# Triangular inverse of the delta rule: doubling levels on stacked 64-blocks instead of full 128-blocks

## The chip, the cores and the metric

The kernel runs on one NeuronCore of one Trainium2 chip. The metric is device time in microseconds (us), from one execution of the whole program. TensorE (PE) does the matrix products, VectorE (DVE) and ScalarE (ACT) the elementwise work, GpSimd (POOL) elementwise work and some DMA issues, SyncE (SP) issues the weight stream. Every matrix product of two float32 operands that this text speaks of shows in the trace as two passes, each one with its own weight load (LDWEIGHTS, the row PEld) and its own matmul record (the row PE).

## The reference, cut to what matters

Two layers of a hybrid block run in a loop, followed by a second block with gated linear attention, a convolution, differential attention and experts. Each of the two layers has a gated delta rule with 4 heads over 256 tokens. Its core is a unit lower-triangular solve:

```python
a_kk = jnp.where(strict, jnp.einsum('bhnid,bhnjd->bhnij', kb, k) * gamma, 0.0)
tri = a_kk + jnp.eye(C, dtype=f32)
rhs = jnp.concatenate([v * beta[..., None], kb * jnp.exp(G)[..., None]], axis=-1)
sol = lax.linalg.triangular_solve(tri, rhs, left_side=True, lower=True, unit_diagonal=True)
```

The kernel works with chunks of 128 tokens, so there are 4 heads x 2 chunks = 8 triangular matrices of 128x128 in each layer, and it builds their inverses. In the same stretch of the program runs the sliding-window attention of 8 heads of 64 features, which has nothing to do with the inverse and is woven into it.

## The kernel before

Weights stream through a ring of three 512 KB tiles; ACT and DVE split each tile into a high and a low part (L1586, L1824) and PE multiplies with three products per tile (L1246 to L1248). These products fill most of the program. Each engine executes its own list of instructions in order, and the lists are tied together by counting semaphores; nothing else sets the order.

The stretch that the change touches is the same in both layers, between the last input projection and the output projection. `bp` holds the 8 matrices (transposed, not yet masked), made by DVE at L2001 from the Gram products in PSUM (L1420) and decay factors times beta, which POOL multiplies at L2161. The inverse is then built by doubling, in `LEVELS` = 7 levels (0 to 6). At level `lev` the inverse of each diagonal block of size 2^lev is known, and blocks of twice the size are made of them:

- POOL makes the level's mask product `bl` (L2171): `bp` times a 0/1 matrix of constants ("level"), 8 matrices of 128x128 in one instruction (two instructions of four at level 0). `bl` has two buffers; from level 2 on POOL waits until level lev-2 is over.
- Level 0: PE turns `bl` (L1461, a product with the identity), DVE takes both `bl` and its turned form from the identity (L2035 and L2037). The results are `uinv` and `tinv`, the inverse and its transpose.
- Levels 1 to 6, first half, called X here: PE forms `bl` times `tinv` (L1470) into banks 6 and 7, ACT copies it to `xs` (L1736).
- Second half, called Y here: PE forms `uinv` times `xs` (L1479, not at level 6) and `xs` times `uinv` (L1481), and DVE subtracts them from `tinv` (L2042) and from `uinv` (L2043).

Each of these steps is done in two groups `g` of four matrices, one PSUM bank each. Between X and Y of each level, PE, DVE and ACT do one step `attend(i)` of the attention: the scores of head i (L1332, L1333, with 64 rows of the array), the transposes of head i-2 (L1327), and the values of head i-3 (L1450 to L1452, with 64 columns of the array). Thus the first two levels carry scores only, level 3 carries transposes too, and from level 4 on all three. After level 6 come the products of the recurrence (L1489 to L1517), again with `attend` steps between them.

POOL has one more piece of work in this stretch: behind the masks of levels 0 and 1 it forms `qg` and `kbg` (L2177 to L2180, twelve instructions) and issues two DMAs for `post_mix` and `post_ffn` (L2185), and only then the mask of level 2. DVE waits on `lev_y` and `tu_ready`, ACT on `lev_x`, PE on `bl_ready`, `tu_ready` and `lev_xs`.

Of the kernel before, what the change touches and what calls it, by code (L numbers as in the profile page):

```python
# [14 lines left out]
P = 128  # L15
# [16 lines left out]
LEVELS = 7  # L32

# [60 lines left out]
def columns(*widths):  # L94
# [10 lines left out]
    ("level", LEVELS * P), ("dilmask", 3 * P), ("causal", 3 * P), ("gmask", P),  # L105
# [50 lines left out]
def block_program(nc, xt, wtiles, consts, packa, packf, packb, packp, out):  # L156
    v, a, pl, t = nc.vector, nc.scalar, nc.gpsimd, nc.tensor
    ctx = ExitStack()
    with ctx:
# [74 lines left out]
        tinv, xs = (sq[:, 4 * i:4 * i + 4, :].rearrange("p a (u k) -> p (a u) k", k=P) for i in range(2))  # L234
        bl = y[:].rearrange("p (w a) (u k) -> p w (a u) k", w=2, k=P)
# [151 lines left out]
        lev_x, lev_xs, lev_y, tu_ready = sem("lev_x"), sem("lev_xs"), sem("lev_y"), sem("tu_ready")  # L387
        rec_pe, rec_act, rec_dve = sem("rec_pe"), sem("rec_act"), sem("rec_dve")
# [850 lines left out]
        def _(pe):  # L1239
# [99 lines left out]
            def layer(l):  # L1339
# [117 lines left out]
                pe.wait_ge(bc_dve, l * 4 + 4)  # L1457
                for g in range(2):
                    pe.wait_ge(bl_ready, l * (LEVELS + 1) + g + 1)
                    for u in range(4):  # L1460
                        mm = t.matmul(bank[g][:, u * P:(u + 1) * P], bl[:, 0, 4 * g + u, :], ident, start=True, stop=True)  # L1461
                    mm.then_inc(lev_x, 1)
                pe.wait_ge(tr_dve, l * 4 + 4)
                pe.wait_ge(tr_act, l * 4 + 4)
                for lev in range(1, LEVELS):
                    pe.wait_ge(bl_ready, l * (LEVELS + 1) + lev + 2)
                    for g in range(2):
                        pe.wait_ge(tu_ready, l * 2 * LEVELS + 2 * (lev - 1) + g + 1)
                        for u in range(4 * g, 4 * g + 4):
                            mm = t.matmul(bank[6 + g][:, u % 4 * P:u % 4 * P + P], bl[:, lev % 2, u, :], tinv[:, u, :],  # L1470
                                          start=True, stop=True)
                        mm.then_inc(lev_x, 1)
                    attend(lev - 1)
                    for g in range(2):

                        pe.wait_ge(lev_xs, l * 2 * (LEVELS - 1) + 2 * (lev - 1) + g + 1)
                        for u in range(4 * g, 4 * g + 4):
                            if lev < LEVELS - 1:
                                t.matmul(bank[g][:, u % 4 * P:u % 4 * P + P], uinv[:, u, :], xs[:, u, :],  # L1479
                                         start=True, stop=True)  # L1480
                            mm = t.matmul(bank[6 + g][:, u % 4 * P:u % 4 * P + P], xs[:, u, :], uinv[:, u, :],  # L1481
                                          start=True, stop=True)
                        mm.then_inc(lev_y, 1)
# [98 lines left out]
        def _(act):  # L1582
# [62 lines left out]
            def layer(l):  # L1645
# [87 lines left out]
                for lev in range(1, LEVELS):  # L1733
                    for g in range(2):
                        act.wait_ge(lev_x, l * 2 * LEVELS + 2 * lev + g + 1)
                        a.activation(xs[:, 4 * g:4 * g + 4, :], bank[6 + g][:, :].rearrange("p (u k) -> p u k", u=4),  # L1736
                                     ACT.Copy).then_inc(lev_xs, 1)
# [82 lines left out]
        def _(dve):  # L1820
# [84 lines left out]
            def layer(l):  # L1905
# [72 lines left out]
                for i in range(DNH + 1):  # L1978
# [14 lines left out]
                    if i < 0:  # L1993
# [7 lines left out]
                    v.tensor_tensor(bp[:, 2 * i:2 * i + 2, :], pair[:, :, 0, :],  # L2001
                                    bp[:, 2 * i:2 * i + 2, :], ALU.mult).then_inc(gram_used, 1)
# [22 lines left out]
                for lev in range(LEVELS):  # L2025
                    if lev >= 1:
                        attend(lev - 1)
                    for g in range(2):
                        us = slice(4 * g, 4 * g + 4)
                        t_ps = bank[g][:, :].rearrange("p (u k) -> p u k", u=4)  # L2030
                        u_ps = bank[6 + g][:, :].rearrange("p (u k) -> p u k", u=4)
                        if lev == 0:
                            eye = ident.unsqueeze(1).to_broadcast([P, 4, P])
                            dve.wait_ge(bl_ready, l * (LEVELS + 1) + g + 1)
# [336 lines left out]
```

## Time and profile before

| | us |
|---|---|
| median of 3 runs | 1341.01 |
| lowest, highest | 1338.49, 1342.27 |
| the profiled execution, its own time | 1337.07 |
| its span, first to last instruction | 1335.3 |
| busy share of the span: PE, DVE, ACT, POOL | 94%, 61%, 50%, 25% |

The rows below come from that profiled execution. Times in it are us from the start of the span. The stretch described above runs from about 122 to 192 us in the first layer and from about 538 to 608 us in the second. The page has a line "PEclk" with the granted clock of TensorE in each of 40 slices of the span, in tenths of full speed: 9 is full speed (2.4 GHz), and a lower digit is a slice in which the clock was at 1.2 GHz for some of the time. In other views the same share is 1.00 or 0.50. The chain of waits is the work that ended last, followed back from the last instruction to what released each step.

### The profile page before, as it was taken

To read this page: it belongs to the slowest core of one execution; us is meant where nothing else is said; L and a number is where in the kernel's file an instruction comes from. 1 tells how busy PE (TensorE), PEld (TensorE's weight loads), DVE (VectorE), ACT (ScalarE), POOL (GpSimd) and SP (SyncE) were. 2 spreads that over 40 slices of the span, in tenths; PEclk is the share of its full clock that TensorE was granted. 3 is DMA by queue.
4 is the path that set the end of the run, shared out by engine and by line. 5 is a ranking of instruction groups with operands and counts; after the bars stand their busy time and mean duration, and the time that the engine had idled before them with its cause. 6 is when DMAs were issued, how large, how long until landed. Compare 5 with 4: busy or idle time off the path is not lost.

```text
span 1335.3 us, 25081 instructions
## 1 busy us (share of the span) xinstructions
PE 1256.9 (94%) x8802; PEld 1163.0 (87%) x8802; DVE 817.2 (61%) x1293; ACT 664.0 (50%) x1085; POOL 328.5 (25%) x370
## 2 busy tenths in 40 slices
PE   8998898999997999899899999888789999999998
PEld 8997787999996999788899998788668889999997
DVE  5666546766666855555766666597355455555554
ACT  6654245655555664345555555583144444444442
POOL 2014301322222001510322222487200122222221
PEclk9999999999999999899999999998559889999999
DMA  6542003555553544003355555233103245555553
GB/s 240 166 152 80 32 4 109 199 187 181 182 188 112 171 147 145 32 1 108 123 181 182 187 188 188 80 127 111 48 1 110 80 142 188 185 182 185 186 187 128
DMA packets 49802, 181.12 MB, mean 136 GB/s; under 512 B 5568, under 2 KB 5728, under 8 KB 49600
## 3 DMA queue, kind: packets, MB, share of 16 engines
q1 hardware_dynamic: 48816, 176.98, 40.0%
q0 software_dynamic: 912, 3.16, 0.7%
q8 instruction: 46, 0.75, 0.2%
q14 instruction: 28, 0.23, 0.1%
HBM read 179.07 MB, written 1.05 MB: 135 GB/s over the span
## 4 chain that ended last, share of the span: by engine, by line
PE 83%; DVE 6%; POOL 4%; ACT 3%; issue 3%; DMA 0%; POOLq 0%; DVEq 0%; ACTq 0%; SPq 0%
PE bank L1246 22%; PE bank L1247 22%; PE bank L1248 22%; PE bank L1481 2%; PE bank L1470 1%; PE bank L1479 1%; PE bank L1305 1%; PE bank L1327 1%; POOL region L1186 1%; PE bank L1296 1%; POOL region L1161 1%; POOL region L1164 1%; PE bank L629 1%; PE bank L1333 1%; ACT w L1586 1%
## 5 line engine op out<-in xcount | busy, mean ns | idle before, releaser
L1824 DVE TENSOR_TENSOR w<-ring,w 128x1024 fp32r<-128x1024 f32 x330 | 412.1, 1250 | 224.4 <-ACT w L1586 224.2
L1246 PE MATMUL bank<-act,w 128*128 128x256 f32 x1728 | 498.8, 289 | 18.0 <-DVE act L1846 8.1
L1247 PE MATMUL bank<-act,w 128*128 128x256 f32 x1728 | 493.8, 286 | 0.0
L1248 PE MATMUL bank<-act,w 128*128 128x256 f32 x1728 | 493.6, 286 | 0.0
L1586 ACT ACTIVATE w<-ring 128x1024 fp32r<-128x1024 f32 x330 | 347.7, 1055 | 188.0 <-PE bank L1248 181.7
L1246 PEld LDWEIGHTS bank<-act,w 128*128 128x128 f32 x1728 | 336.6, 195 | 25.2 <-issue 11.3
L1247 PEld LDWEIGHTS bank<-act,w 128*128 128x128 f32 x1728 | 336.9, 195 | 2.3
L1248 PEld LDWEIGHTS bank<-act,w 128*128 128x128 f32 x1728 | 336.4, 195 | 0.0
L2094 DVE SCALAR_TENSOR_TENSOR region<-bank,pf,region 128x255 f32<-128x255 f32 (+1 forms) x176 | 84.8, 482 | 74.8 <-ACT region L1787 63.7
L1246 PE MATMUL bank<-w,hid 128*128 128x512 f32 x304 | 119.3, 393 | 3.9 <-POOL hid L2196 2.0
L1247 PE MATMUL bank<-w,hid 128*128 128x512 f32 x304 | 118.9, 391 | 0.0
L1248 PE MATMUL bank<-w,hid 128*128 128x512 f32 x304 | 118.3, 389 | 0.0
L1787 ACT ACTIVATE region<-bank,pf 128x256 f32<-128x256 f32 x88 | 49.6, 563 | 132.4 <-PE bank L1248 132.2
L2193 POOL TENSOR_TENSOR region<-region 128x256 f32<-128x256 f32 x44 | 65.0, 1478 | 180.7 <-DVE region L2094 146.9
L2142 POOL TENSOR_TENSOR h<-act 128x256 f32<-128x256 f32 x48 | 38.4, 839 | 257.5 <-DVE act L1846 257.4
L1246 PE MATMUL bank<-w,act 128*128 128x256 f32 (+1 forms) x208 | 71.9, 346 | 1.2 <-DVE w L1824 1.2
L1246 PEld LDWEIGHTS bank<-w,hid 128*128 128x128 f32 x304 | 57.3, 188 | 15.5 <-POOL hid L2196 2.8
L1247 PE MATMUL bank<-w,act 128*128 128x256 f32 (+1 forms) x208 | 69.6, 335 | 0.0
L1248 PE MATMUL bank<-w,act 128*128 128x256 f32 (+1 forms) x208 | 69.6, 335 | 0.0
L1248 PEld LDWEIGHTS bank<-w,hid 128*128 128x128 f32 x304 | 57.1, 188 | 12.3
L1247 PEld LDWEIGHTS bank<-w,hid 128*128 128x128 f32 x304 | 57.3, 188 | 9.7
L1199 POOL TENSOR_TENSOR region<-region 128x256 f32<-128x256 f32 x32 | 24.7, 772 | 154.7 <-DVE region L1110 154.7
(329 smaller groups left out, 1648.9 us busy)
## 6 DMA issues: line engine op xcount, KB each, us to landing
ring<-wtiles SPq DMA_DIRECT2D x330, 512.0 KB, 3.3
region<-packp POOLq DMA_DIRECT2D x4, 512.0 KB, 4.1
cst<-consts SPq DMA_DIRECT2D x1, 1348.0 KB, 11.6
x<-xt SPq DMA_DIRECT2D x2, 512.0 KB, 5.7
out<-x SPq DMA_DIRECT2D x4, 256.0 KB, 2.1
pa<-packa POOLq DMA_DIRECT2D x3, 285.5 KB, 3.8
pb<-packb SPq DMA_DIRECT2D x1, 260.5 KB, 10.8
cst<-consts SPq DMA_DIRECT2D x1, 192.5 KB, 2.6
```

Of the source, the lines that this page charges most:

```text
L629: mm = t.matmul(bank[6 + i % 2][:, j * S:(j + 1) * S], ident[0:NE, 2 * i + j:2 * i + j + 1].to_broadcast([NE, P]), gate_t[0:NE, :], start= ...
L1199: pl.tensor_tensor(e_prod[:, j, :], e_act[:, j, :], e_up[:, j, :], ALU.mult).then_inc(ex_prod, 1)
L1246: t.matmul(out_, still[:, 0], moving[:, 0], start=first, stop=False)
L1247: t.matmul(out_, still[:, 0], moving[:, 1], start=False, stop=False)
L1248: return t.matmul(out_, still[:, 1], moving[:, 0], start=False, stop=last)
L1481: mm = t.matmul(bank[6 + g][:, u % 4 * P:u % 4 * P + P], xs[:, u, :], uinv[:, u, :], start=True, stop=True)
L1586: a.activation(w_hi[:, s, :], ring[:, s, :], ACT.Copy).then_inc(hi_ready, 1)
L1787: a.activation(dst[:, q, :], bank[UP_BANKS[2 * q + w]][:, 0:S], ACT.Identity, scale=pf_("conv", p * 6 + w * 3 + 2), bias=pf_("bias", p * 2 ...
L1824: v.tensor_tensor(w_lo[:, s, :], ring[:, s, :], w_hi[:, s, :].bitcast(F32), ALU.subtract).then_inc(lo_ready, 1)
L2094: ins = v.scalar_tensor_tensor(dst[:, q, j:], src[:, 0:S - j], pf_("conv", p * 6 + w * 3 + 2 - j), dst[:, q, j:], ALU.mult, ALU.add)
L2142: pl.tensor_tensor(h[:, k, :], act_hi[:, k, :].bitcast(F32), act_lo[:, k, :].bitcast(F32), ALU.add).then_inc(h_ready, 1)
L2193: pl.tensor_tensor(glu_p[:, q, :], glu_a[:, q, :], glu_v[:, q, :], ALU.mult).then_inc(prod_done, 1)
```

## The change

The change takes the 128x128 matrices as two diagonal 64x64 blocks and the block above the diagonal in `bp`. Levels 0 to 5 never leave the diagonal blocks, so they are done on the two blocks alone, which are stacked: rows 0 to 63 hold the first block, rows 64 to 127 the second, and each matrix is 64 columns wide. Only level 6 joins the two.

- `by_halves` replaces the four products of a group by eight products of 64x64x64, alternately with rows 0 to 63 into columns 0 to 63 of the array (`low`) and with rows 64 to 127 into columns 64 to 127 (`high`). The first product of each group is wider: it uses the rows of `low` and the columns of both halves, so it fills all 128 rows of its part of the bank, and the next product overwrites the upper half of that.
- The masks of POOL, the copies of ACT and the subtractions of DVE are half as wide, 64 columns per matrix.
- A third buffer, `ublk`, holds the stacked inverse; at level 5 DVE writes its halves to their places in `uinv` (three instructions per group in place of two), and POOL has zeroed the left half of `uinv` with a new memset in front of the level 0 masks.
- Level 6 has no mask. X is one 64x64x64 product per matrix, straight from `bp`, and Y one product per matrix in place of one 128x128x128. DVE then writes one 64x64 block per matrix with its sign turned.
- DVE's product L2001 becomes two instructions, one for each half of the rows, so that the lower half lands in columns 0 to 63.
- POOL's `qg`, `kbg` and the two DMAs move from behind the mask of level 1 to behind that of level 3.
- The constants "level" shrink from 896 to 384 columns, and "eye" adds 64.

```diff
+                def by_halves(b, g, still, moving, halves=(low, high)):
+                    for u in range(4 * g, 4 * g + 4):
+                        at = slice(u % 4 * HB, (u % 4 + 1) * HB)
+                        for p in halves:
+                            if u == 4 * g and p == low:
+                                mm = t.matmul(b[:, at], still[p, u:u + 2, :].rearrange("p u k -> p (u k)"), moving(p, u),
+                                              start=True, stop=True)
+                            else:
+                                mm = t.matmul(b[p, at], still[p, u, :], moving(p, u), start=True, stop=True)
+                    return mm
...
-                for lev in range(1, LEVELS):
-                    pe.wait_ge(bl_ready, l * (LEVELS + 1) + lev + 2)
+                for lev in range(1, LEVELS - 1):
+                    pe.wait_ge(bl_ready, l * LEVELS + lev + 2)
                     for g in range(2):
                         pe.wait_ge(tu_ready, l * 2 * LEVELS + 2 * (lev - 1) + g + 1)
-                        for u in range(4 * g, 4 * g + 4):
-                            mm = t.matmul(bank[6 + g][:, u % 4 * P:u % 4 * P + P], bl[:, lev % 2, u, :], tinv[:, u, :],
-                                          start=True, stop=True)
-                        mm.then_inc(lev_x, 1)
+                        by_halves(bank[6 + g], g, bl[:, lev % 2], lambda p, u: tinv[p, u, :]).then_inc(lev_x, 1)
                     attend(lev - 1)
                     for g in range(2):
-
                         pe.wait_ge(lev_xs, l * 2 * (LEVELS - 1) + 2 * (lev - 1) + g + 1)
...
+                        by_halves(bank[g], g, ublk, lambda p, u: xs[p, u, :], (low,) if lev == LEVELS - 2 else (low, high))
+                        by_halves(bank[6 + g], g, xs, lambda p, u: ublk[p, u, :]).then_inc(lev_y, 1)
+
+                for g in range(2):
+                    pe.wait_ge(tu_ready, l * 2 * LEVELS + 2 * (LEVELS - 2) + g + 1)
+                    for u in range(4 * g, 4 * g + 4):
+                        mm = t.matmul(bank[6 + g][:, u % 4 * HB:(u % 4 + 1) * HB], bp[low, u, :], tinv[low, u, :],
+                                      start=True, stop=True)
+                    mm.then_inc(lev_x, 1)
+                attend(LEVELS - 2)
+                for g in range(2):
+                    pe.wait_ge(lev_xs, l * 2 * (LEVELS - 1) + 2 * (LEVELS - 2) + g + 1)
+                    for u in range(4 * g, 4 * g + 4):
+                        wide = u < 4 * g + 3
+                        mm = t.matmul(bank[6 + g][slice(0, P) if wide else low, u % 4 * HB:(u % 4 + 1) * HB],
+                                      xs[high, u:u + 2, :].rearrange("p u k -> p (u k)") if wide else xs[high, u, :],
+                                      uinv[high, u, high], start=True, stop=True)
+                    mm.then_inc(lev_y, 1)
...
-                    v.tensor_tensor(bp[:, 2 * i:2 * i + 2, :], pair[:, :, 0, :],
-                                    bp[:, 2 * i:2 * i + 2, :], ALU.mult).then_inc(gram_used, 1)
+                    two = slice(2 * i, 2 * i + 2)
+                    v.tensor_tensor(bp[0:HB, two, :], pair[0:HB, :, 0, :], bp[0:HB, two, :], ALU.mult)
+                    v.tensor_tensor(bp[HB:P, two, 0:HB], pair[HB:P, :, 0, HB:P], bp[HB:P, two, HB:P],
+                                    ALU.mult).then_inc(gram_used, 1)
...
+                pl.memset(uinv[:, :, 0:HB], 0.0).then_inc(corner_zero, 1)
+                for lev in range(LEVELS - 1):
...
-                    for i in range(DNH) if lev == 1 else ():
+                    for i in range(DNH) if lev == 3 else ():
```

On PE, from level 0 of a layer to the first products of level 1's Y. In the kernel before, `y` is the mask product `bl`, `sq` is `tinv` or `xs`, `region` is `uinv`, `h` is the attention's input, and `cst` the identity; each MATMUL row is one product of two passes:

```order
L1461 MATMUL bank<-cst,y 128x128 x8
L1468 ISA
L1470 MATMUL bank<-sq,y 128x128 x4
L1468 REGISTER_ALU
L1470 MATMUL bank<-sq,y 128x128 x4
L1332 MATMUL bank<-h 128x128
L1333 MATMUL bank<-h 128x256
L1476 ISA
L1479 MATMUL bank<-sq,region 128x128
L1481 MATMUL bank<-region,sq 128x128
```

The same place in the changed kernel, where `sq` is `tinv`, `xs` or `ublk`, and L1470 is the wide product that opens each group:

```order
L1484 ISA
L1470 MATMUL bank<-sq,y 128x64
L1473 MATMUL bank<-sq,y 64x64 x7
L1484 REGISTER_ALU
L1470 MATMUL bank<-sq,y 128x64
L1473 MATMUL bank<-sq,y 64x64 x7
L1335 MATMUL bank<-h 128x128
L1336 MATMUL bank<-h 128x256
L1488 ISA
L1470 MATMUL bank<-sq 128x64
L1473 MATMUL bank<-sq 64x64 x7
```

Each group of four products is now one wide product and seven small ones; the `attend` step stands where it stood, and Y follows it with four such groups where it had sixteen alternating products.

On POOL, from the last product of decay and beta to the mask of level 3, before:

```order
L2161 TENSOR_TENSOR region<-region 128x256
L2171 TENSOR_TENSOR y<-region,cst 128x512 x2
L2171 TENSOR_TENSOR y<-region,cst 128x1024
L2177 TENSOR_TENSOR region<-region 128x128
...
L2185 DMA region<-packp 128x1024
L2166 ISA
L2171 TENSOR_TENSOR y<-region,cst 128x1024
L2166 REGISTER_ALU
L2171 TENSOR_TENSOR y<-region,cst 128x1024
```

and in the changed kernel, where L2208 is the mask product and L2214 the first instruction of `qg`:

```order
L2197 TENSOR_TENSOR region<-region 128x256
L2199 MEMSET region 128x8x64
L2208 TENSOR_TENSOR y<-region,cst 128x256 x2
L2208 TENSOR_TENSOR y<-region,cst 128x512
L2203 ISA
L2208 TENSOR_TENSOR y<-region,cst 128x512
L2203 REGISTER_ALU
L2208 TENSOR_TENSOR y<-region,cst 128x512
L2214 TENSOR_TENSOR region<-region 128x128
```

The memset is new, the masks are half as wide, and the masks of levels 2 and 3 now stand ahead of the twelve `qg` and `kbg` instructions and the two DMAs.

## Rows read from the trace of the kernel before

**Rows 1.** The page: granted clock in 40 slices, and the chain by engine.
```profile
PEclk9999999999999999899999999998559889999999
...
PE 83%; DVE 6%; POOL 4%; ACT 3%; issue 3%; DMA 0%; POOLq 0%; DVEq 0%; ACTq 0%; SPq 0%
```

**Rows 2.** Groups by line, 120 to 180 us; count | busy us, mean ns | idle before.
```profile
L2171 POOL TENSOR_TENSOR y<-region,cst 128x1024 f32<-128x1024 f32 (+1 forms) x8 | 14.5, 1828 | 19.8 <-DVE region L2043 12.0 <-PE bank L1470 7.8
...
L1470 PE MATMUL bank<-sq,y 128*128 128x128 f32 x96 | 14.4, 302 | 6.7 <-POOL y L2171 4.4 <-DVE region L2043 2.3
...
L2043 DVE TENSOR_TENSOR region<-region,bank 128x512 f32<-128x512 f32 x12 | 8.2, 682 | 0.8 <-PE bank L1481 0.8
...
L2161 POOL TENSOR_TENSOR region<-region 128x256 f32<-128x256 f32 x3 | 2.2, 723 | 3.5 <-ACT region L1705 3.5
...
L1999 DVE TENSOR_TENSOR region<-bank,region 128x256 f32<-128x256 f32 x3 | 1.3, 425 | 0.3
```

**Rows 3.** The chain in order of time, 110 to 200 us: start, length, what.
```profile
138.12 3.42 PE bank L1470 x16
...
156.31 0.42 PE bank L1332 x2
...
157.63 0.36 PE bank L1450 x2
...
158.43 0.42 PE bank L1479 x2
...
159.29 0.22 PE bank L1481 x2
...
177.45 0.41 PE bank L1332 x2
```

**Rows 4.** PE timeline in both layers: start, length, what [idle before <- releaser].
```profile
124.92 2.11 PE L1461 MATMUL bank<-cst,y 128*128 128x128 f32 x16 [2.37 <-POOL y L2171]
...
155.15 1.16 PE L1470 MATMUL bank<-sq,y 128*128 128x128 f32 x8 [0.57 <-DVE region L2043]
163.67 1.16 PE L1470 MATMUL bank<-sq,y 128*128 128x128 f32 x8 [0.57 <-DVE region L2043]
...
541.02 3.75 PE L1461 MATMUL bank<-cst,y 128*128 128x128 f32 x16 [2.37 <-POOL y L2171]
...
592.08 0.48 PE L1332 MATMUL bank<-h 64*128 64x128 f32 x2
```

**Rows 5.** PE timeline of the second block: rows*columns of the array, then moving data.
```profile
916.96 1.09 PE L1305 MATMUL bank<-cst,region 128*64 128x128 f32 x16
...
965.48 0.80 PE L1332 MATMUL bank<-h 64*128 64x128 f32 x4
...
854.03 3.63 PE L452 MATMUL bank<-h,pb 128*16 128x256 f32 x16
...
1061.61 10.06 PE L629 MATMUL bank<-region,cst 16*128 16x256 f32 x32 [0.46 <-ACT region L804]
```

**Rows 6.** Busy time by stretch: stretch, us, PE busy (records), granted clock, DMA share, GB/s.
```profile
541.00:544.00 3.00, 2.98 (x14) 0.50 0.00 0
...
1062.70:1066.00 3.30, 3.30 (x17) 1.00 0.00 0
1066.10:1072.50 6.40, 5.57 (x14) 0.50 0.00 0
...
975.00:990.00 15.00, 13.95 (x47) 0.50 0.01 2
```

**Rows 7.** The chain in order of time, 976 to 990 us, at the lower clock.
```profile
986.74 0.64 PE bank L557 x2
987.37 0.43 PE bank L558 x2
...
988.22 0.72 PE bank L1332 x2
988.95 0.87 PE bank L1333 x2
```

More of the change, by code:

```diff
@@ L32 @@
 LEVELS = 7
+HB = P // 2
 GH, GDK, GDV, GRANK, GTAU = 4, 32, 64, 16, 16.0
@@ L232, in block_program @@
         qkn = qkvc[:, 0:8, :]
-        tinv, xs = (sq[:, 4 * i:4 * i + 4, :].rearrange("p a (u k) -> p (a u) k", k=P) for i in range(2))
-        bl = y[:].rearrange("p (w a) (u k) -> p w (a u) k", w=2, k=P)
+        tinv, xs, ublk = (sq[:, 2 * i:2 * i + 2, :].rearrange("p a (u k) -> p (a u) k", k=HB) for i in range(3))
+        bl = y[:, 0:4, :].rearrange("p (w a) (u k) -> p w (a u) k", w=2, k=HB)
         ar = Arena(region, ARENA)
@@ L1457, in layer @@
                 pe.wait_ge(bc_dve, l * 4 + 4)
+                low, high = slice(0, HB), slice(HB, P)
+                def by_halves(b, g, still, moving, halves=(low, high)):
[8 more added lines that the diff above has]
+                    return mm
                 for g in range(2):
[L1459 to L1462 removed]
+                    pe.wait_ge(bl_ready, l * LEVELS + g + 1)
+                    by_halves(bank[g], g, bl[:, 0], lambda p, u: ident[p, p]).then_inc(lev_x, 1)
                 pe.wait_ge(tr_dve, l * 4 + 4)
                 pe.wait_ge(tr_act, l * 4 + 4)
[L1465 to L1466 removed]
+                for lev in range(1, LEVELS - 1):
+                    pe.wait_ge(bl_ready, l * LEVELS + lev + 2)
                     for g in range(2):
                         pe.wait_ge(tu_ready, l * 2 * LEVELS + 2 * (lev - 1) + g + 1)
[L1469 to L1472 removed]
+                        by_halves(bank[6 + g], g, bl[:, lev % 2], lambda p, u: tinv[p, u, :]).then_inc(lev_x, 1)
                     attend(lev - 1)
@@ L2242, in shape_constants @@
     levels = []
-    for lev in range(LEVELS):
+    col = np.arange(HB)[None, :]
+    row = i[:, None] % HB
+    for lev in range(LEVELS - 1):
         b = 2 ** lev
-        same = i[:, None] // (2 * b) == i[None, :] // (2 * b)
-        levels.append(same & (i[:, None] % (2 * b) < b) & (i[None, :] % (2 * b) >= b))
+        levels.append((row // (2 * b) == col // (2 * b)) & (row % (2 * b) < b) & (col % (2 * b) >= b))
     put("level", np.concatenate(levels, axis=1))
+    put("eye", row == col)
     times = np.zeros((S, S))
```

44 lines of the change are left out of this document (24 added, 20 removed).

## The prediction

> **What bounds the kernel now.** I read the page first: PE holds 83% of the chain [rows 1], so what this change does to the time is what it does to PE's list, and to the moments in which PE waits for DVE or POOL. The grouped lines of 120 to 180 us come next: ahead of L1470 PE was idle for 6.7 us in the first layer, 4.4 of them behind POOL's mask L2171 and 2.3 behind DVE's L2043 [rows 2]. Last the chain and the timeline. A product of 128x128x128 costs 0.22 us, two passes of 0.11 [rows 3]. A level with all its attention repeats every 8.52 us (163.67 - 155.15), with one idle piece of 0.57 us, in front of the second group of X [rows 4]. So the levels are bound by PE, and DVE adds a little in each. From level 0 to the first attention step behind level 6 a layer takes 52.5 us in the first layer (177.45 - 124.92) [rows 3, 4] and 51.1 us in the second (592.08 - 541.02) [rows 4].
>
> **PE, one group of products.** Before: four products, 8 x 0.11 = 0.89 us, at no other cost, since the array's configuration stays 128x128 from product to product. The reader is to see what a change of configuration costs: the first L1479 behind the 64-column products takes 0.42 where its followers take 0.22, so 0.20; the first L1450, into 64 columns, takes 0.36, so 0.14 [rows 3]. After: one wide product (64 rows, 128 columns) and seven of 64x64. Whether 64x128 to 64x64 costs as much stands in no row: the ends are 0 and 0.20, I take 0.20 into the wide one and 0.14 out of it, the nearest rows. The Trainium skill, "TensorEngine Tiling (Array Packing)", Key Properties, says that changing the tiling mode drains TensorE, and changing the tile does not. The rows agree with the first half.
>
> Do opposite quarters run side by side? Sixteen L1305 passes of 128 moving columns on alternating column halves take 1.09 us with the drain of the last, where 16 x 0.11 would be 1.76: about 0.055 each; two scores on the two row halves (four L1332 passes) take 0.80 us [rows 5] where one takes 0.72 at the same lower clock [rows 7]. So both kinds of halves overlap. A quarter's pass has 64 moving columns, 0.055 us, and two share that time: 14 passes cost 14 x 0.0275 = 0.39 us; without overlap 0.77. The group: 0.20 + 0.22 + 0.14 + 0.39 = **0.95 us** against 0.89 before. From the bounds: 0.61 to 1.33. There are 30 such groups in a layer: 2 at level 0, 6 in each of levels 1 to 4, 4 at level 5, whose other two have half the small products but all on one quarter (0.20 + 0.22 + 0.14 + 6 x 0.055 = 0.89).
>
> **DVE, ACT, POOL, with the clock at full speed.** DVE's two subtractions per group fall from 0.68 each to about 0.43 (L1999 has the new size) [rows 2]. What follows the last product of a level then takes 0.86 us and some 0.35 of latency, 1.2, in place of 1.36 + 0.35 = 1.7; PE covers 0.95 of it with the first group of X. The wait shrinks from some 0.85 us (0.57 idle, plus the fill behind it) to 0.2, PE's list grows by 0.16 to 0.2: -0.45 us per level for levels 2 to 5. ACT's copy is covered by the attention, before and after. Level 6: X is 16 passes of 0.055 on one quarter (0.9 against 1.8), but waits for three DVE instructions; Y is two groups of 1.07 against 1.98: together -0.5.
>
> POOL: the masks halve (L2171, 1.83 on average, towards L2161's 0.72 for 128x256 [rows 2]), and the mask of level 2 no longer queues behind twelve products and two DMAs. The 4.4 us of waiting for POOL go, and with them the low clock behind it, 3.42 us for 16 passes that need 1.8 [rows 3]: 4.4 + 1.6 = 6.0, of which 0.4 is due again to DVE: -5.6. For the second layer, where the clock was already low at level 0 (3.75 against 2.11 us for 16 passes [rows 4]), I take -4.5, between 1.6 and 5.6. `qg`, `kbg` and the DMAs, moved behind mask 3, hold up only mask 4, by less than 12 x 0.72 us (L2161 is twice their size) and about 1 us of DMA issue; it is due two levels later, 13 us or more: covered. The new memset has no row; between 0 and 1.4 us (twice L2161), I take 0.5, and the first mask, half as wide, gives about as much back. L2001 in two costs DVE 0.3 four times, in gaps behind PE; uncovered it would be 1.2 us per layer. The smaller constants land early either way.
>
> Sum at full clock: -5.6 - 4.5 - 2 x (4 x 0.45 + 0.5) = **-14.7 us**.
>
> **The clock.** This decides the sign. PE waits 2.37 us ahead of level 0 in both layers [rows 4], and the change leaves that wait. Behind it the granted clock was 0.50 in the second layer (541 to 544 us) [rows 6], and in the first it fell in the next wait [rows 3]. What brought it back in the kernel before was a row of full 128x128 products with no gap, and the second layer lost almost nothing. After the change there is none in the levels: what follows the wait uses 64 rows or a quarter, with a change of configuration in each group. Which kind of work holds the clock? L629, 16 rows of the array by 128 columns, ran without a gap (busy 3.30 of 3.30 us at 1.00), and the clock fell to 0.50 behind that [rows 5, 6]. L452, 128 rows by 16 columns, kept full speed, 0.22 us for a pass of 256 columns [rows 5]. And from 975 to 990 us, scores on 64 rows with small products between them, PE shows busy for 13.95 of 15 us and the clock stays at 0.50 [rows 6]. The levels of the changed kernel are nearest to that last row. I forecast that the clock falls by level 1 in both layers and returns only with the full products of the recurrence.
>
> At the lower clock a product of 128 columns takes 0.43 (L558), the way into 64 rows costs 0.72 - 0.43 = 0.29, the way out of it 0.64 - 0.43 = 0.21 [rows 7], and a group 0.29 + 0.43 + 0.21 + 7 x 0.107 = **1.68 us**. An attention step: scores 0.72 + 0.87 = 1.6; with transposes 2.4; with values (0.64 + 0.43 + 0.43) 3.9. Levels 1 to 4: 4 x 6 x 1.68 + 1.6 + 1.6 + 2.4 + 3.9 = 49.8. Level 5: 4 x 1.68 + 3.9 + 2 x 1.57 = 13.8. Level 6: 2.3 + 3.9 + 4.0 = 10.2. Level 0: 2.1 to 3.4. The sum is 76 us in the first layer and 77.3 in the second: +23.5 and +26.2 against 52.5 and 51.1. Two more attention steps and 24 passes of the recurrence run at the lower clock before it returns: 13.2 against 7.3 us, +5.9 in each. DVE's waits vanish behind the longer groups. Total **+61.5 us**: 1337.1 + 61.5 = 1398.6 for the profiled execution. The median lies 3.9 above it, so 1402.5.
>
> **Rivals.** (1) *The clock holds, or returns at once.* Then the sum at full clock stands: 1341.0 - 14.7 = 1326.3 (1312 with free configuration changes, 1335 with dear ones). For it: POOL's wait, the longest in the levels, is gone, and PE has fewer gaps. Against it: L629. It decides from the point at which the products behind the 2.37 us wait bring the clock back. The Trainium skill, "TensorE: Matmul & The Clock Gate", names the monitor one of how busy PE is and advises against idle gaps; by busy share alone this rival would win. The L629 rows speak against reading busy time so. (2) *The clock is low in one layer only, or the change from wide to quarter is free.* One layer: 1402.5 less 29.4 and 7.4, 1366. Free: 30 x 0.5 x 2 = 30 less, 1372. (3) *Opposite quarters don't overlap, because they write one bank.* The score pair wrote two banks, so no row excludes it. At full clock 30 x 0.385 less the waits covered, 10.5 a layer: 1347. At the lower clock 0.75 x 60 = 45 more: 1447. The Trainium skill, "TensorEngine Tiling (Array Packing)", Gotcha 1, says that different row tiles cannot access the same PSUM bank at once. By that rule this rival is the case, where row tiles in different columns count as such; no row here shows it. (4) *The change does not shorten what I think, nor slow the clock:* the masks were never late and the levels cost the same, 1341.
>
> **How the numbers follow.** Low clock in both layers 0.52; rival 1 0.24; rival 2 0.14; rival 3 0.04 at the low and 0.03 at the full clock; rival 4 0.03. The forecast is the likeliest case, 1402, with a range of its own of 1378 (clock back a level or two early, or groups of 1.5 us) to 1425 (groups of 1.85). Cases of both signs hold weight, so the range runs from 1318 to 1422, which leaves out the dearest of rival 3 and the ends of the others. A measurement of this kernel tells some 0.3%, 4 us, from no change. Slower: 0.52 + 0.14 + 0.04 and part of rival 3, 0.71. Faster: 0.24. Same: 0.05.
>
> **What the profile would show.** The granted clock of both stretches: 0.50 from about 127 and 543 us to about the recurrence, or 1.00. The group of eight products: 0.95 us at full or 1.68 at the lower clock, a step of 0.1 to 0.2 at each wide product, small ones starting in pairs. L1470's waits for the mask gone. DVE's subtractions 0.43. If the clock stays at 1.00 my forecast is wrong from that step on, and the time should be near 1326; if small products start one by one, the overlap step was wrong.

## The result, and the profile after

| | before | after |
|---|---|---|
| median | 1341.64 us (4 runs, 1338.49 to 1342.67) | 1391.88 us (4 runs, 1390.43 to 1392.62) |
| ratio | | 1.0394, 95% interval 1.037 to 1.0417 |
| profiled execution, span | 1337.1, 1335.3 us | 1390.4, 1388.7 us |
| mean granted clock | 0.957 | 0.904 |

The change costs 50 us, 3.9%. The page of the kernel after shows where: the granted clock over 40 slices, and the chain by engine.

```profile
PEclk9998559999999999757999999999757989999999
...
PE 85%; DVE 5%; POOL 4%; ACT 3%; issue 2%; DMA 0%; POOLq 0%; DVEq 0%; ACTq 0%; SPq 0%
```

Against [rows 1] two dips are new, from the fourth to the sixth slice and from the seventeenth to the nineteenth. Those are the two layers' levels. The timeline of PE there (start, length, instructions [idle before <- releaser]):

```profile
125.36 0.43 PE L1470 MATMUL bank<-cst,y 64*128 64x64 f32 x2 [2.29 <-POOL y L2208]
125.72 0.99 PE L1473 MATMUL bank<-cst,y 64*64 64x64 f32 x14
126.74 0.68 PE L1470 MATMUL bank<-cst,y 64*128 64x64 f32 x2
...
128.39 0.68 PE L1470 MATMUL bank<-sq,y 64*128 64x64 f32 x2
...
200.20 0.79 PE L1335 MATMUL bank<-h 64*128 64x128 f32 x2
...
570.04 0.68 PE L1470 MATMUL bank<-cst,y 64*128 64x64 f32 x2 [2.28 <-POOL y L2208]
...
643.52 0.49 PE L1335 MATMUL bank<-h 64*128 64x128 f32 x2
```

The wait ahead of level 0 is the one of [rows 4], 2.3 us. Behind it the joined product of 64 rows by 128 columns (L1470) goes from 0.43 to 0.68 us, in the first layer within one group. In the second the clock had fallen in the wait itself, and the first joined product already takes 0.68. From there a group of eight products takes 1.65 us (126.74 to 128.39). The busy time by stretch (stretch, us, PE busy (records), granted clock, DMA share, GB/s) shows the clock that goes with it:

```profile
134.00:180.00 46.00, 46.00 (x405) 0.50 0.07 24
180.00:208.00 28.00, 28.00 (x133) 0.50 0.00 1
570.00:641.00 71.00, 70.96 (x565) 0.50 0.05 16
648.00:660.00 12.00, 12.00 (x93) 0.99 0.01 2
```

For 46 us PE has no idle time at all, and the clock does not return. In the first layer it does so at 211 us, at the recurrence's second group of products on the full array (L1518). In the second it is back at 641 us, behind the attention step of level 6 and ahead of the recurrence, though the same instructions had not brought it back in the first. Y of level 6 (L1503) shows the difference:

```profile
196.47 3.81 PE L1503 MATMUL bank<-region,sq 64*128 64x64 f32 x16
...
641.40 2.20 PE L1503 MATMUL bank<-region,sq 64*128 64x64 f32 x16
```

Before the change, the stretch from 134 to 180 us had PE busy for 40.8 us, at a clock of 0.96.

Where the 53.4 us between the two profiled executions lie, read from the starts of level 0, of the first scores behind level 6 and of the first weight product behind the recurrence (L1246 before, L1249 after):

| | before | after | difference |
|---|---|---|---|
| first layer, level 0 to the scores behind level 6 | 52.5 | 74.8 | +22.3 |
| from there to the first weight product | 15.2 | 20.3 | +5.1 |
| second layer, the same two | 51.1, 15.2 | 73.5, 16.8 | +22.4, +1.6 |
| all the rest | | | +2.0 |

DVE's and POOL's work became smaller, as the grouped lines from 127 to 190 us show (count | busy us, mean ns | idle before):

```profile
L2208 POOL TENSOR_TENSOR y<-region,cst 128x512 f32<-128x512 f32 x5 | 5.4, 1088 | 25.6 <-DVE sq L2071 24.3 <-PE bank L1473 1.3
...
L2070 DVE TENSOR_TENSOR sq<-sq,bank 128x256 f32<-128x256 f32 x8 | 3.4, 421 | 18.9 <-PE bank L1473 18.9
L2071 DVE TENSOR_TENSOR sq<-sq,bank 128x256 f32<-128x256 f32 x8 | 3.3, 414 | 0.0
```

A mask of levels 1 and up takes 1.09 us (2.07 before; the 1.83 of [rows 2] is a mean over two widths), a subtraction 0.42 (0.68), and both wait for PE.

### The profile page after: what moved, and what is told of

It is laid out like the page before. It is cut to its first block, busy times and chain, and to the rows that moved or that the text cites. A ratio compares the mean times of both kernels' runs of the same rounds, so it can differ in the third digit from the quotient of the medians.

```text
span 1388.7 us, 26063 instructions
## 1 busy us (share of the span) xinstructions
PE 1320.3 (95%) x9282; PEld 1207.5 (87%) x9282; DVE 805.2 (58%) x1305; ACT 659.7 (48%) x1085; POOL 313.3 (23%) x370
## 4 chain that ended last, share of the span: by engine, by line
PE 85%; DVE 5%; POOL 4%; ACT 3%; issue 2%; DMA 0%; POOLq 0%; DVEq 0%; ACTq 0%; SPq 0%
PE bank L1249 22%; PE bank L1250 21%; PE bank L1251 21%; PE bank L1473 5%; PE bank L1470 3%; PE bank L1330 1%; PE bank L1308 1%; PE bank L1336 1%; POOL region L1189 1%; PE bank L1299 1%; PE bank L1335 1%; POOL region L1164 1%; POOL region L1167 1%; PE bank L632 1%; ACT w L1609 1%
## 5 line engine op out<-in xcount | busy, mean ns | idle before, releaser
L1249 PE MATMUL bank<-act,w 128*128 128x256 f32 x1728 | 499.3, 289 | 18.0 <-DVE act L1871 8.2
L1249 PEld LDWEIGHTS bank<-act,w 128*128 128x128 f32 x1728 | 337.1, 195 | 25.0 <-issue 11.3
L1249 PE MATMUL bank<-w,hid 128*128 128x512 f32 x304 | 119.3, 393 | 3.9 <-POOL hid L2233 2.0
L1249 PE MATMUL bank<-w,act 128*128 128x256 f32 (+1 forms) x208 | 71.9, 346 | 1.2 <-DVE w L1849 1.2
L1249 PEld LDWEIGHTS bank<-w,hid 128*128 128x128 f32 x304 | 57.3, 188 | 15.6 <-POOL hid L2233 2.8
```

The costliest lines, as they stand in the source:

```text
L1249: t.matmul(out_, still[:, 0], moving[:, 0], start=first, stop=False)
```

## The experiments

All ratios are to the kernel before, run beside each kernel on the same chip; its median there was 1338.1 to 1338.3 us. In the runs with a name in `a_` the base is the changed kernel, in those with `b_` the kernel before. "Full products" are the existing `keep_warm`: the identity by a tile of ones, 128x128x128, with an unused result. The time of such a run is that of the kernel's own work and of these products.

**Does the wait or do the products lower the clock?** The forecast held both for part of the cause; these two runs separate them.

```
 # a_warm, PE ahead of level 0
 pe.wait_ge(bc_act, l * 4 + 4)
 pe.wait_ge(bc_dve, l * 4 + 4)
+keep_warm(10)
```

> The changed kernel with ten full 128x128 products, whose result is not used, between the wait for the decay copies and level 0, so that TensorE is not idle ahead of level 0. Theory P (the shapes of the products let the clock fall): the granted clock still falls to 0.50 within the levels, time 1385 to 1392. Theory W (the clock falls in the wait of 2.3 us, and the levels would keep what they find): the clock stays at 1.00, time 1322 to 1340.

Measured: 1334.29 us (10 runs, 1331.3 to 1338.03), ratio 0.9963 (0.9943 to 0.9982). Ten products whose result nobody uses take 58 us away from the changed kernel. Its PE timeline:

```profile
124.70 2.47 PE L1316 MATMUL bank<-cst 128*128 128x128 f32 x20
127.10 0.43 PE L1471 MATMUL bank<-cst,y 64*128 64x64 f32 x2
...
155.43 0.43 PE L1471 MATMUL bank<-sq 64*128 64x64 f32 x2
155.80 0.68 PE L1474 MATMUL bank<-sq 64*64 64x64 f32 x14
156.40 0.43 PE L1471 MATMUL bank<-sq 64*128 64x64 f32 x2
```

Its busy time by stretch, columns as above:

```profile
127.00:166.00 39.00, 38.66 (x547) 1.00 0.08 29
...
539.00:576.00 37.00, 36.66 (x521) 1.00 0.09 31
578.00:593.00 15.00, 15.00 (x64) 0.50 0.00 0
```

The same products that sat at 0.50 run here at 1.00 for 39 and 37 us, in both layers; a group takes 0.97 us (155.43 to 156.40). So theory W holds for levels 0 to 4: without the wait, these shapes do not lower the clock. The ten products do two things at once, they close the wait and they add full-array work ahead of level 0; the run `a_warm_oldpool` below separates the two. At the end of level 5 or in level 6 the clock still falls, at 167 us behind 0.40 us of idle time, at 577 us, in the last group of level 5, with none ahead of it.

```
 # a_back: the wait stays; full products between level 0 and level 1
+pe.wait_ge(tu_ready, l * 2 * LEVELS + 2)
+keep_warm(16)
 for lev in range(1, LEVELS - 1):
```

> The changed kernel with its wait ahead of level 0 left as it is, and sixteen full 128x128 products with an unused result between level 0 and level 1. Theory H (the levels keep the clock that they find; they neither lower it nor bring it back): the clock is 0.50 in level 0, comes back within the sixteen products and stays at 1.00 to level 5. Against the run without idle time (1334.3) a layer pays level 0 at the lower clock, 1.7 us, the products at 0.43 us each as far as the clock is low, 5 to 7 us, and about 1 us for DVE's part of level 0: 1350 to 1354. Rival (only a TensorE that was never idle keeps the clock; once it has fallen, the levels lower it again): 1392 plus 14 us of added products, 1400 to 1406.

Measured: 1351.2 us (5 runs, 1346.5 to 1354.93), ratio 1.0086 (1.0055 to 1.0116), within theory H. PE's timeline:

```profile
128.11 0.68 PE L1470 MATMUL bank<-cst,y 64*128 64x64 f32 x2
128.72 1.11 PE L1473 MATMUL bank<-cst,y 64*64 64x64 f32 x14
130.35 6.68 PE L1316 MATMUL bank<-cst 128*128 128x128 f32 x32 [0.52 <-DVE sq L2067]
136.96 0.43 PE L1470 MATMUL bank<-sq,y 64*128 64x64 f32 x2
```

And by stretch:

```profile
127.00:130.00 3.00, 2.83 (x31) 0.50 0.00 0
130.00:137.00 7.00, 6.65 (x33) 0.55 0.01 2
137.00:170.00 33.00, 33.00 (x468) 1.00 0.09 34
```

The clock fell in the wait as in the changed kernel. Sixteen full products brought it back near their end, and then the levels kept it for 33 us. Levels 1 to 4 thus kept the clock that they found: at 1.00 they held it, at 0.50 they did not raise it.

**How much idle time does it take?** `a_warm4` is `a_warm` with `keep_warm(4)`.

> The changed kernel with four full products instead of ten in the wait ahead of level 0, so that about 1.4 us of idle time is left of 2.3. Theory (the length of the idle piece decides): the shorter piece does not lower the clock and the time is that of the run with ten, 1332 to 1338. Rival (any piece of idle time ahead of these products lowers it, in both layers): 1385 to 1392; in one layer only, 1360 to 1366.

Measured: four executions, three at 1393.91 to 1395.45 us and one at 1359.29 (mean clock 0.90 and 0.93). The profiled one is of the three; PE's timeline:

```profile
126.86 0.43 PE L1471 MATMUL bank<-cst,y 64*128 64x64 f32 x2 [1.16 <-POOL y L2209]
...
128.24 0.43 PE L1471 MATMUL bank<-cst,y 64*128 64x64 f32 x2 [0.34 <-POOL y L2209]
...
129.38 0.43 PE L1471 MATMUL bank<-sq,y 64*128 64x64 f32 x2
129.73 1.03 PE L1474 MATMUL bank<-sq,y 64*64 64x64 f32 x14
130.69 0.68 PE L1471 MATMUL bank<-sq,y 64*128 64x64 f32 x2
```

A piece of 1.16 us and one of 0.34 are enough: two groups and a half run at full speed behind the first of them, then the clock goes, in both layers of this execution. My theory that the shorter piece would be harmless is wrong. The odd execution lies just under the time that I had worked out for a fall in one layer only (1360 to 1366); it has no trace.

**What the POOL order is worth.** `b_pool` is the kernel before with that part of the change alone:

```
-for i in range(DNH) if lev == 1 else ():
+for i in range(DNH) if lev == 3 else ():
...
-if lev == 1:
+if lev == 3:
```

> The kernel before with one part of the change alone: GpSimd's products of `qg` and `kbg` and its two DMA issues stand behind the mask of level 3 instead of level 1; products, masks, copies and subtractions keep their full width. Theory (the prediction's term for POOL): the late mask went because of the order, so some 8 to 10 us go: about 1332, with the wait of L1470 for POOL shorter in both layers. Rival: the late mask went because the masks are half as wide; the order alone gives nothing, 1339 to 1342.

Measured: 1333.36 us (8 runs), ratio 0.9945 (0.9924 to 0.9967): 7.4 us less, 4.4 to 10.2. The wait for the mask of level 2 (2.92 us in the first layer, 1.70 in the second) is gone; that is what the order did. The 1.45 us ahead of level 1 in the first layer are gone too, but not by the order, as the next run shows. The wait of 2.37 us ahead of level 0 remains, and now it lowers the clock in the first layer too, where before it had not [rows 4]. The row of PE's timeline:

```profile
126.29 3.65 PE L1461 MATMUL bank<-cst,y 128*128 128x128 f32 x16 [2.37 <-POOL y L2171]
```

That is one profiled execution of each kernel. `b_pool_warm` adds `keep_warm(10)` to it.

> The kernel before with GpSimd's block behind the mask of level 3 and ten full products in the wait ahead of level 0. Theory: as without the ten products, less the stretch at low clock in the second layer (3.75 us for 16 passes that take 2.11 in the first) and in the first: 1 to 4 us less than that run, 1328 to 1331, and the fastest kernel so far. Rival: the ten products delay level 0 by as much as the clock gives back, no difference between the two.

Measured: 1331.89 us (7 runs), ratio 0.9943 (0.9921 to 0.9965). That can't be told from `b_pool`, as the rival said, though the ten products did keep the clock at 1.00 in both layers. The two traces show where the gain went. PE's first products of level 1, in `b_pool` and in `b_pool_warm`:

```profile
129.85 2.10 PE L1470 MATMUL bank<-sq,y 128*128 128x128 f32 x16
...
130.21 2.10 PE L1471 MATMUL bank<-sq,y 128*128 128x128 f32 x16 [1.45 <-POOL y L2172]
```

POOL's mask of level 1, still 128 columns wide per matrix, sets their start: they begin 6.3 us behind the start of the last product ahead of the wait (L1421) in both kernels (123.53 and 123.88 us). In `b_pool` level 0 at the lower clock fills that time, in `b_pool_warm` level 0 takes 2.18 us and PE waits for the mask. So the fall at level 0 of `b_pool` costs nothing: the clock is back by the end of level 0, and the mask is not there sooner.

In the changed kernel the order decides more. `a_warm_oldpool` is `a_warm` with the two conditions back at level 1:

> The changed kernel with ten full products ahead of level 0 and GpSimd's block of `qg`, `kbg` and two DMA issues back behind the mask of level 1, as in the kernel before. Theory (the order of GpSimd's work is most of its term, 7 us in the kernel before): the mask of level 2 is late by 12 products of some 0.3 us and two DMA issues; TensorE waits some 2 to 4 us in each layer: 1339 to 1343 if the clock holds, 1360 to 1390 where the wait lowers it in one layer or both. Rival (with masks half as wide the order does not matter): 1334.

Measured: 1383.6 us (4 runs, 1383.28 to 1383.73), ratio 1.0334 (1.0317 to 1.0352), 49 us more than `a_warm`. PE's timeline holds the whole case in three rows:

```profile
135.25 0.67 PE L1474 MATMUL bank<-sq 64*64 64x64 f32 x14
137.97 0.68 PE L1471 MATMUL bank<-sq,y 64*128 64x64 f32 x2 [2.04 <-POOL y L2209]
138.58 1.11 PE L1474 MATMUL bank<-sq,y 64*64 64x64 f32 x14
```

The stretches ahead of that wait and behind it:

```profile
127.00:137.90 10.90, 8.58 (x133) 0.94 0.10 27
137.90:180.00 42.10, 42.03 (x349) 0.50 0.05 19
```

The late mask costs 2 us of idle time, and some 22 us a layer by the clock that it takes along. This run has the ten full products of `a_warm` and differs from it only in POOL's order, which for PE is that one wait. So it is the idle time that lowers the clock, and not a want of full products ahead of the levels.

**Do opposite quarters overlap?** `a_warm_serial` is `a_warm` with the loops of `by_halves` exchanged:

```
-for u in range(4 * g, 4 * g + 4):
-    at = slice(u % 4 * HB, (u % 4 + 1) * HB)
-    for p in halves:
+for p in halves:
+    for u in range(4 * g, 4 * g + 4):
+        at = slice(u % 4 * HB, (u % 4 + 1) * HB)
```

> The changed kernel with ten full products ahead of level 0, and in each group first all products of the low rows, then all of the high rows, so that no two neighbours lie in opposite quarters. Theory (opposite quarters overlap, though they write one bank): a group takes 0.20 + 0.22 + 0.14 + 6 x 0.055 + 8 x 0.055 = 1.33 us in place of 0.96, 56 groups: 20 us more, 1350 to 1358. Rival (no overlap in either order, or overlap hidden elsewhere): a group of 0.96 as now, 1334.

Measured: three executions of 1348.5 to 1349.3 us and three of 1371.6 to 1379.5; the ratio by the faster three is 1.0069 (1.0033 to 1.0105). The profiled one is of the slower three, with its second layer at full clock. There a group reads in PE's timeline:

```profile
581.47 0.43 PE L1471 MATMUL bank<-sq,y 64*128 64x64 f32 x2
581.83 0.84 PE L1474 MATMUL bank<-sq,y 64*64 64x64 f32 x14
582.61 0.43 PE L1471 MATMUL bank<-sq,y 64*128 64x64 f32 x2
```

The joined product and the way out of it take 0.36 us in both orders, the fourteen small passes 0.78 here and 0.60 in `a_warm`. A group is 1.14 us against 0.97. So quarters in opposite corners do run side by side although they write one bank. The starts of the single records say it directly: in `a_warm` twelve of the fourteen passes begin in six pairs, the two of a pair 6 to 7 ns apart, and a pair follows the last mostly by 58 ns. I had expected a group of 1.33: the serial order is not fully serial either, since at the change from the low to the high rows three pairs of passes begin within 6 ns (582.00, 582.11 and 582.17 us), which is three passes, or 0.17 us, less than one after the other. The faster three executions lie just under the range of 1350 to 1358. In the first layer the clock fell with no wait before it, as its stretches show:

```profile
127.00:130.00 3.00, 3.00 (x47) 1.00 0.02 5
130.00:135.00 5.00, 5.00 (x42) 0.61 0.00 0
135.00:180.00 45.00, 45.00 (x343) 0.50 0.07 24
```

Work that fills one quarter at a time can lose the clock without any idle time; in this run it did in one layer and not in the other.

**What a group's parts cost, and a faster kernel.** Call Y's two halves T, `ublk` times `xs` for `tinv`, and U, `xs` times `ublk` for the inverse itself. In `a_warm_uq` the U groups of levels 1 to 5 lose the joined product. They follow the T groups without a wait, so their quarters go on where T's end:

```
 # a_warm, and in by_halves (new argument joined=True):
-if u == 4 * g and p == low:
+if joined and u == 4 * g and p == low:
 ...
-by_halves(bank[6 + g], g, xs, lambda p, u: ublk[p, u, :]).then_inc(lev_y, 1)
+by_halves(bank[6 + g], g, xs, lambda p, u: ublk[p, u, :], joined=False).then_inc(lev_y, 1)
```

> The changed kernel with ten full products ahead of level 0, and the U groups of levels 1 to 5 (ten in a layer) made of eight pairs of quarters, without the product of 64 rows by 128 columns at their head, so that the configuration does not change there. Theory (a group of 0.97 us is 0.36 for that product and the way into it, 0.15 of the way out, and eight pairs of 0.058): 0.5 us less per group, 20 groups, 10 us less where TensorE sets the pace, less by DVE's subtractions where they come out: 1322 to 1330, against 1334.3. Rival (more work in quarters and less in wider shapes lowers the clock within the levels, as in the run with serial quarters): 1350 to 1385 with the clock at 0.50 in one layer or both.

Measured: 1321.3 us (4 runs, 1314.65 to 1330.04), ratio 0.9871 (0.9816 to 0.9925), 13 us less than `a_warm` and the lowest median of all. Its profiled execution held 1.00 to the end of level 5 in both layers (in the first PE was busy for 32.34 of 33.00 us from 127 to 160) and lost the clock in level 6 of the first, from 163.4 to 173.8 us. T and U of one half of the heads in PE's timeline:

```profile
144.09 1.14 PE L1474 MATMUL bank<-sq 64*64 64x64 f32 x30
145.17 0.43 PE L1471 MATMUL bank<-sq 64*128 64x64 f32 x2
```

Thirty small passes take 1.08 us where fourteen take 0.60: a group of eight products without the joined one costs 0.48 us, half of one with it. A level with all its attention repeats every 6.96 us (143.73 to 150.69), in `a_warm` every 7.96, in the kernel before every 8.52. A version with no joined product at all was not tried.

**The end of the levels.** `a_warm_end` puts two full products ahead of T of level 5 and of X and Y of level 6, which use one quarter or one row half for most of their products; `a_warm_uq_end` puts three there, on top of `a_warm_uq`.

```
# X of level 6; the same two lines stand ahead of the other groups. 3 in a_warm_uq_end
+for _ in range(2):
+    t.matmul(bank[6 + g][:, S:S + P], ident, ones, start=True, stop=True)
 for u in range(4 * g, 4 * g + 4):
     mm = t.matmul(bank[6 + g][:, u % 4 * HB:(u % 4 + 1) * HB], bp[low, u, :], ...
```

> The changed kernel with ten full products ahead of level 0 and, besides, two full products ahead of each of the six groups that work on one quarter or on one row half: T of level 5, X and Y of level 6. Without these the clock fell there, at about 167 and 577 us, and was back at about 177 and 594 us; low stretches of some 6.8 and 17 us by the granted clock cost about 3.4 and 8.5 us. Theory (those one-sided groups lower the clock, full products among them keep it): 1.00 through both layers' levels, 12 us less and 24 products of 0.22 us more, 5.3: 1326 to 1329. Rival (the clock falls there whatever is added): 1334 plus 5 or more, 1339 to 1345.

> As the run without the joined product in the U groups, and three full products ahead of each of the six one-sided groups of levels 5 and 6. Theory: 18 products a layer, 4.0 us, 2 us of it ahead of level 6 beside DVE's work; it keeps the clock at 1.00 through level 6 in most executions and gives back 3.4 and 8.5 us: 1 to 5 us below the run without them. Rival (the clock falls earlier, within levels 1 to 5): equal to the run without them plus 8 us.

Measured: 1332.64 us (6 runs, 1329.15 to 1338.77), ratio 0.9951 (0.9928 to 0.9975), and 1324.83 us (6 runs, 1320.72 to 1333.72), ratio 0.9914 (0.9877 to 0.9951). Neither can be told from the kernel it was made from. With two products the profiled execution kept 1.00 in the first layer and lost it in level 6 of the second (0.50 from 580 to 590 us); with three it kept it in both. The expected gains did not come; what the clock gave back is within what the added products (5 and 8 us) took.

**Full products in every group.** `a_fill4` is `a_warm` with four full products at the head of each call of `by_halves`.

> As the run with ten products ahead of level 0, and four full 128x128 products with an unused result ahead of each group of 64-blocks, 32 groups a layer. Theory P (what matters to the clock is how much full-array work lies in the levels): the clock stays at 1.00. The added work is 256 products of 0.22 us, 57 us, on top of the sum at full clock of 1326: 1375 to 1392 us, so as fast as the changed kernel although it does 57 us more; a group of products 0.89 + 0.95. Rival (the low clock has another cause that the shapes don't touch): 256 products of 0.43 us, 110 us, on top of 1392: about 1500 us at 0.50.

Measured: 1403.66 us (4 runs, 1402.22 to 1407.86), ratio 1.0464 (1.0427 to 1.0502). Its clock is 1.00 from 125 to 200 us. The time is above the 1375 to 1392 that I expected because the four take 1.09 us and not 0.89 (in the timeline from 143.86 to 144.95, a group in all 2.05): each four pay the way out of the quarters.

64 times 1.09 is 70 us, and 1334.3 + 70 = 1404.

## Why the prediction was right, point by point

The forecast was 1402.5 us, the measurement 1391.9; the sign, the place and the low clock as the cause were right. The stated range, 1318 to 1422, covers the faster kernel of rival 1 as well and so proves little by itself; what came true is the likeliest case of 0.52. Between the profiled executions the sum was 8 us too high, 61.5 against 53.4: 10 too much in the two layers, and 2.0 us elsewhere that it did not have.

- **The bound.** PE holds the chain, 85%. Held.
- **The group of products.** Forecast 0.95 us at full and 1.68 at the lower clock; measured 0.97 (`a_warm`) and 1.65. The split holds as well: 0.36 for the joined product and the way out, 0.60 for fourteen overlapping passes and the way in. That a change from 64x128 to 64x64 costs as much as one from 128x128, for which no row stood, is borne out by this and by `a_warm_uq`. The small passes start in pairs, as forecast.
- **DVE.** Forecast 0.43 us and 0.45 less per level; measured 0.42, and 0.56 less per level (8.52 to 7.96). The wait of [rows 4] in front of the second X group is gone.
- **POOL.** Forecast 10.1 us for both layers; the order alone gave 7.4 (4.4 to 10.2) on the kernel before. The forecast counts the narrower masks too, and the 1.45 us ahead of level 1 hang on them and not on the order. The memset: forecast 0.5 us, measured 0.53. The block behind mask 3 held up nothing: in `a_warm` the mask of level 4 ends at 146.5 us and is used from 149.4. In the changed kernel itself the term lies under PE's slow work; `a_warm_oldpool` shows what it is worth there, 49 us, which I had not seen.
- **The sum at full clock**, 1326.3. `a_warm` gave 1334.3 with low stretches of 6.8 and 17 us left at levels 5 and 6, which cost half their length, 12 us. Without them it would be 1322, by that estimate; against the medians run beside each, that is -14.7 us forecast and -16 by the estimate.
- **The clock falls in the wait and returns with the recurrence.** The fall is right in both layers, the return in the first; in the second the clock came back one attention step early, ahead of level 6's Y. **The reason that I gave for it was wrong in one step**: "The levels of the changed kernel are nearest to that last row", the 13.95 busy us of 15 at 0.50 from 975 to 990 us [rows 6]. That row had the clock low from its start. It shows that such work does not raise the clock, which was true here. It does not show that such work would lose it, and `a_warm` and `a_back` show that it doesn't. The row was also read wrongly as scores "with small products between them". Here are groups of that stretch:

```profile
L1332 PE MATMUL bank<-h 64*128 64x128 f32 x8 | 3.2, 498 | 0.0
L1327 PE MATMUL bank<-cst,region 128*128 128x128 f32 x7 | 2.3, 444 | 0.8 <-DVE region L981 0.8
...
L557 PE MATMUL bank<-region 128*128 128x128 f32 x4 | 1.6, 497 | 0.6 <-ACT region L751 0.6
```

With L558 and L559, four passes each, 19 of its 47 records are full 128x128x128 passes. So it is not near to levels of quarters; it says that some full products among others do not always raise the clock. L629 [rows 5, 6], the other witness, is work that lost it, behind 0.46 us of idle time; level 6 and the serial order are of its kind, the levels are not. So that the levels don't bring the clock back came true, and that they lose it did not. One more reading was off: in the first layer of the kernel before, the clock fell not in the next wait but in the one after it. The 1.45 us ahead of level 1 left it at 1.00, the 2.92 us ahead of level 2 did not (0.50 from 138 us).
- **Rival 1** named the right deciding point, whether the products behind the 2.37 us wait bring the clock back. They don't. The Trainium skill, "TensorE: Matmul & The Clock Gate", calls the gate's monitor one of how busy PE is (Terms) and advises against idle gaps between bursts of matmuls (Why this matters for your kernels). The second half fits nearly every run here: each fall in levels 0 to 4 stands behind idle time of 1.2 to 2.9 us, but for that of `a_warm_serial`; the gaps that the page warns of are longer than these. By the first half, the 46.00 busy us of 46.00 in the changed kernel should have raised the clock, and it stayed at 0.50. The trace disagrees there.
- **Stages at the lower clock** (first layer, forecast and measured): level 0 2.1 to 3.4, 3.0; levels 1 to 4 49.8, 48.2; level 5 13.8, 13.4; level 6 10.2, 10.2. In the last a term was mis-sized: X of level 6 was put at 0.055 us a pass at full clock, as a product on one quarter. The list of changes above calls it 64x64x64 too, but L1495 takes all 128 columns of `bp` as weights: it is a product of 64 rows by 128 columns, like the joined one, which the prediction had at 0.11 a pass. Its passes take twice the forecast, as the last three start 0.21 to 0.22 us apart at the lower clock; sixteen are 3.4 us and not the 2.3 that I gave X with its wait. The first scores run beside the last of them, and Y took 3.7 us instead of 4.0, so the stage came out the same. The rows of PE's timeline:

```profile
192.79 0.42 PE L1495 MATMUL bank<-sq,region 64*128 64x64 f32 x1
...
193.01 0.42 PE L1495 MATMUL bank<-sq,region 64*128 64x64 f32 x1
...
193.22 0.42 PE L1495 MATMUL bank<-sq,region 64*128 64x64 f32 x1
```

- **The recurrence.** Forecast +5.9 in each layer; measured +5.1 and +1.6. In the second layer the clock was back by level 6's Y, before the recurrence, and low again only from 645 to 648 us. With the second layer's levels (73.5 against the 77.3 forecast) that makes 8 of those 10 us; the first layer makes the other 2.
- **Rival 3**, no overlap within a bank. Wrong, by `a_warm_serial` and by the starts in pairs. The Trainium skill, "TensorEngine Tiling (Array Packing)", Gotcha 1, says that different row tiles can't access one PSUM bank at once; the low rows wrote the low half of the partitions, the high rows the high half of the same bank, and they overlapped, 0.60 against 0.78 us. The trace disagrees with the page here.

## What to carry to other kernels

A change that makes TensorE's work smaller has to be judged at both clocks. Here the small products are as good as the large at full clock (0.97 against 0.89 us a group) and nearly twice as dear at the lower one (1.65 us). Large products are as dear there, 3.42 us for two groups [rows 3], but in the kernel before they had the clock back within 7 us, and the small ones did not bring it back in 46 us. So each wait of a microsecond or two ahead of them should be found and closed first; ten unused products in it were worth 58 us. Once that is done, keep the array's configuration for as long as possible: the joined product at the head of a group cost as much as eight quarter products. And a row of a trace in which the clock is low from the start says what doesn't raise it, not what lowers it.

## What the runs showed of the hardware that was not expected

- The same work can sit at either clock. The levels of 64x64 products ran at 1.00 for 39 us (`a_warm`) and at 0.50 for 46 us without idle time (after), the same instructions in the same order.
- The return is not certain either. Behind X of level 6 and its attention step the clock came back in the second layer of the changed kernel (641 us) and in the first of `a_warm` (171 us) and of `a_warm_oldpool` (195 us); in the first layer of the changed kernel and the second of `a_warm` it did not. What decides it stays open.
- Idle time of 1.16 us and 0.34 behind it was enough for a fall in both layers in three executions of four by their times, one of them seen in the trace; in the kernel before 2.37 us did not lower the clock in the first layer and did in the second. So the fall behind such a wait is not certain, and this stays open too.
- Work on one quarter or one row half lost the clock without idle time: the end of level 5 at 577 us in `a_warm`, and one layer of `a_warm_serial`. Full products between it helped in one layer of two (two of them) or in both (three of them), in one profiled execution each; that is too little to call it settled.
- A pass with 64 moving columns and 128 weight columns is no shorter than one with 128 moving columns: 0.21 to 0.22 us at the lower clock for both. The weight columns seem to set it; no run changed them alone.
